# A fused two-block transformer kernel: order of the sparse attention's units, its softmax and two modulation sums beside the output projection

## The chip, the cores and the metric

The kernel runs on one core of one Trainium2 chip. The metric is device time in microseconds (us) of the whole program. A core has a tensor engine (PE, with its weight loads shown as PEld), a vector engine (DVE), a scalar engine (ACT), GpSimd (POOL, hardly used here) and a queue that issues loads (SP). Each engine runs its own list of instructions in order; they meet at semaphores.

## What is computed

Two transformer blocks over 256 tokens of width 1024, all in fp32. Only the first block's mixer matters here:

```python
mod = silu(c) @ ada_w + ada_b
sh1, sc1, g1, sh2, sc2, g2 = split(mod, 6)
h = rmsnorm(x, norm_mix_w) * (1 + sc1) + sh1
proj = h @ w_in                       # hq hf hi hg | sq sk sv iq ik iw | cu
o_a = hgrn2_mixer(...)                # recurrence, 512 wide
o_b = dsa_mixer(...)                  # top-64 keys per query, 4 heads of 64: 256 wide
o_c = conv_module(cu, ...)            # GLU, 31-tap causal conv, LayerNorm, swish: 256 wide
x = x + g1 * (concat([o_a, o_b, o_c]) @ w_out)
h = rmsnorm(x, norm_mlp_w) * (1 + sc2) + sh2
x = x + g2 * (square(relu(h @ mlp_w1)) @ mlp_w2)
```

In `dsa_mixer` a mask (`sel_bias`) with the 64 selected keys of each query is added to the scaled logits, and a softmax over the keys follows. The gate `g2` is needed only when the MLP's output is added.

## The kernel before

**Products.** A matrix product in fp32 is made from three products of rounded halves (`product3`, lines 582, 587 and 588): high by high, high by low, low by high. A weight tile of 128 x 2048 words arrives in one of five `raw` buffers. ACT rounds it into `w_hi` (line 1122, three buffers, called through `ahead`), and DVE makes `w_lo` as the difference (line 1514, called through `lo_ahead`). PE's `tile` waits for `weights_split`. `ahead(name, by)` makes the tiles up to `by` behind `name`. The activations are split in the same way by `split_input` (lines 1531 and 1532), and `split_mixed(j)` does it for quarter j of the concatenated mixer output `mixT`: quarters 0 and 1 are the recurrence, 2 is the sparse attention, 3 is the convolution.

**PSUM.** Eight banks. `PLAN` lists every result in the order in which PE makes it, and gives it a bank. PE's `begin(key)` waits until the former content of that bank has been read. `psum_full` counts results in the order of the plan. In the part with the convolution the banks go round; `wo` (the output projection) then holds banks 0 to 3, and the attention's results use banks 4 to 7.

**Modulation.** `modulation(u)` multiplies the silu of c with two `ada` tiles on PE (line 674) into a bank; `mod_copy(u)` on ACT copies it out; `modulation_sum(u)` adds the four partial rows up on PE (line 685 for u = 10, 11); `modulation_row(u)` on DVE adds the bias (line 1625). u = 10 and 11 are the two halves of g2. The queue SP loads the next weight tile into a `raw` buffer once its former tile was used: `wo0.1`, `wo1.0`, `wo1.1` and `m1_0.0` take the buffers of `ada20` to `ada23`, which modulations 10 and 11 read.

**The stretch in question**, at about 218 to 305 us:

- PE: convolution half 0 (line 857), modulations 10 and 11, convolution half 1, its mean (865), transposes of the recurrence (871), its variance `cvar` (877), the two modulation sums (685), then the attention beside the projection, `row_half("wo", 2, None)`, the transposes of the MLP's input (657) and the MLP's `m1` tiles.
- The attention has four units i: units 0 and 1 are query block 0 (128 keys), units 2 and 3 query block 1 (256 keys), each with two heads. L is the logits (782), T the transposes of the probabilities (764), O their product with the values (771). "rows j half" are 12 products of the projection with quarter j; quarters run in the order 0, 1, 3, 2, since quarter 2 needs all four O. PE's order before: L0, L1, rows 0 and 1 (48 products), L2, T0, L3, T1, O0, T2, O1, T3, O2, rows 3 first half, O3, rows 3 second half, rows 2.
- DVE: for each unit the mask is added (1588), the maximum taken (1592), and the reciprocal of the sum (1596); O is copied to `mixT` (1631). Around them: the convolution's mean (1832) and square (1835), `cvar` plus epsilon (1843), the splits of quarters 0 and 1, its LayerNorm (1851 to 1856), `modulation_row` 10 and 11 (1625), its product with the sigmoid (1863), the split of quarter 3 in step 1 of the softmax.
- ACT: the taps of the convolution (1193), the copies of the convolution's halves (1286, 1292), the exponentials (1147), the division by the sum (1157), the copy of T (1170).

After quarter 2 DVE splits two weight tiles and adds the projection to x (`gated_residual`, lines 1871 and 1875); the norm and the MLP follow.

Of the kernel before, what the change touches and what calls it, by code (L numbers as in the profile page):

```python
# [24 lines left out]
ALU = mybir.AluOpType  # L25
ACT = mybir.ActivationFunctionType
AX = mybir.AxisListType

P = 128
# [110 lines left out]


ROW_STAGES = {"wo": (0, 1, 3, 2), "o0": (2, 3, 0, 1), "o1": (0, 1, 2, 3)}
DSA_ROWS = [(1, 0, 0), (1, 0, 1), (1, 1, 0), (1, 1, 1), (5, 3, 0), (6, 3, 1)]
MLA_ROWS = [(2, 2, 0), (3, 2, 1), (4, 3, 0), (6, 3, 1), (8, 0, 0), (9, 0, 1)]
FOX_ROWS = [(9, 0, 0), (10, 0, 1), (12, 1, 0), (13, 1, 1), (16, 2, 0), (17, 2, 1)]

# [40 lines left out]
def psum_plan():  # L187
# [38 lines left out]
    for s in range(9):  # L226
# [6 lines left out]
        if 2 <= s <= 7:  # L233
            one(("mod", s + 2), PART_BANKS)
    plan.extend([("sc", t, j) for t in range(TT) for j in range(4)])
    plan.extend([("hgo", 0), ("hgo", 1)])
    plan.extend([("conv", 0), ("mod", 10), ("mod", 11), ("conv", 1), ("cmean",), ("hgt", 0), ("hgt", 1), ("cvar",),
                 ("ms", 10), ("ms", 11)])
    within(range(BANKS))

    def beside_rows(stage, order):
# [4 lines left out]
            plan.append((stage, t, n))  # L246
            banks_of.append(ROW_BANKS[i])

    beside_rows("wo", unit_order("dsa", 4, DSA_ROWS))
    transposes("mlp")  # L250
    for i in range(8):
        gemm(f"m1_{i}")
# [53 lines left out]
def bank(*key):  # L306
    return PLAN_BANKS[USE[key]]
# [7 lines left out]
def build(nc, x_in, wstream, pcol_in, prow_in, const_in, p_in, out):  # L315
    ctx = ExitStack()
    with ctx:
# [236 lines left out]
        def _(pe):  # L554
# [295 lines left out]
            for c in range(2):  # L850
                if c:
                    modulation(10)
                    modulation(11)
                pe.wait_ge(taps_made, c + 1)
                b = begin("conv", c)
                for j in range(31):
                    last = mm(b[:, 0:T], tap_matrix(c, j), hpad[:, c * 286 + j:c * 286 + j + T],
                              start=j == 0, stop=j == 30)
                last.then_inc(psum_full, 1)
# [7 lines left out]
            for t in range(TT):  # L867
                pe.wait_ge(o_normed, t + 1)
                b = begin("hgt", t)
                for h in range(4):  # L870
                    last = nc.tensor.transpose(b[:, h * P:(h + 1) * P],
                                               q_hg[:, t * 512 + h * P:t * 512 + (h + 1) * P], ident)
                last.then_inc(psum_full, 1)
            pe.wait_ge(conv_sq_ready, 1)
            b = begin("cvar")
            for c in range(2):
                last = mm(b[:, 0:T], avg[:, :], conv[:, c * T:(c + 1) * T], start=c == 0, stop=c == 1)
            last.then_inc(psum_full, 1)
            modulation_sum(10)
            modulation_sum(11)  # L880
            in_sbuf("sqk", 0)
            in_sbuf("sqk", 1)
            in_sbuf("sv")
            attention("dsa", 4, two_in_rows(sqT, skT),
                      lambda h, m: sv[:, m * T + h * 64:m * T + (h + 1) * 64], probs_ready, 0,
                      unit_order("dsa", 4, DSA_ROWS), "wo")
            row_half("wo", 2, None)

            to_feature_form("mlp", 2)
            for i in range(8):  # L890
# [173 lines left out]
        def _(act):  # L1064
# [22 lines left out]
            def warm_root(n):  # L1087
                A(table_use[:, n:n + 1], ones[:, 0:1], ACT.Sqrt)
# [36 lines left out]
            def bank_of(name, *key):  # L1125
# [8 lines left out]
                    ahead(name)  # L1134
                return wait_full(*key)

            def softmax(name, heads, base, beside=None):

                us = units(heads)
                for i in range(len(us) + 2):  # L1140
                    if i < len(us):
                        K = (us[i][2] + 1) * P
                        act.wait_ge(logits_ready, base + i + 1)
                        m = 2 * (i % 4)
                        for hh in range(2):
                            L = unit_logits[i % 4][:, hh * K:(hh + 1) * K]
                            last = A(L, L, ACT.Exp, bias=negmax[:, m + hh:m + hh + 1],  # L1147
                                     accum_out=rowsum[:, m + hh:m + hh + 1])
                        last.then_inc(exp_done, 1)
                    if 0 <= i - 1 < len(us):  # L1150

                        K = (us[i - 1][2] + 1) * P
                        m = 2 * ((i - 1) % 4)
                        act.wait_ge(rinv_ready, base + i)
                        for hh in range(2):
                            L = unit_logits[(i - 1) % 4][:, hh * K:(hh + 1) * K]
                            last = A(L, L, ACT.Copy, scale=rinv[:, m + hh:m + hh + 1])
                        last.then_inc(probs_ready, 1)
                    if i >= 2:
                        transposed(name, us, i - 2)  # L1160
                    if beside:
                        beside(i)
# [123 lines left out]
            done(A(conv[:, 0:T], b[:, 0:T], ACT.Identity, bias=col("cv_b", 0)), "conv", 0)  # L1286
            ahead("hi.1", 1)
            mod_copy(10)
            mod_copy(11)
            ahead("hi.1", 2)  # L1290
            b = wait_full("conv", 1)
            done(A(conv[:, T:2 * T], b[:, 0:T], ACT.Identity, bias=col("cv_b", 1)), "conv", 1)
            warm_root(15)
            act.wait_ge(bank_read[bank("cvar")], read("cvar"))
            A(hpad[:, 0:T], hpad[:, 0:T], ACT.Sqrt).then_inc(root_ready, 1)
            act.wait_ge(conv_scaled, 1)
            for c in range(2):
                last = A(conv_d[:, c * T:(c + 1) * T], conv[:, c * T:(c + 1) * T], ACT.Sigmoid)
            last.then_inc(conv_sig_done, 1)
            row_tile_at = {1: "wo0.0", 4: "wo0.1"}  # L1300
            softmax("dsa", 4, 0, lambda i: ahead(row_tile_at[i]) if i in row_tile_at else None)

            def residual_squares(first):
                for i in range(4):
# [182 lines left out]
        def _(dve):  # L1487
# [68 lines left out]
            def rms_norm(n, pieces=1):  # L1556
# [9 lines left out]
                        .then_inc(xn_ready, 1)  # L1566
                own(xn_ready, TT)

            def softmax(name, heads, base, bias, scale, c0, beside, tiles):
                us = units(heads)  # L1570
                n = len(us)
                for i in range(n + 3):
                    if name == "fox" and 1 <= i <= 6:
                        lo_ahead(f"{FOX_UPPER[i - 1][0]}.{FOX_UPPER[i - 1][1]}")
                    if i < n:
                        g, par, t = us[i]
                        K = (t + 1) * P
                        m = 2 * (i % 4)
                        b = wait_full(name, "L", i)
                        L = unit_logits[i % 4][:, 0:2 * K].rearrange("p (h k) -> p h k", h=2)  # L1580
                        if name == "fox":
                            for hh in range(2):
                                h = 4 * g + par + 2 * hh
                                last = V.scalar_tensor_tensor(out=L[:, hh, :], in0=b[:, hh * K:(hh + 1) * K],
                                                              scalar=dtok[:, t * 16 + h:t * 16 + h + 1],
                                                              in1=bias(t), op0=ALU.add, op1=ALU.add)
                        else:
                            last = V.scalar_tensor_tensor(
                                out=L, in0=b[:, 0:2 * K].rearrange("p (h k) -> p h k", h=2), scalar=scale,
                                in1=bias(t).unsqueeze(1).to_broadcast([P, 2, K]), op0=ALU.mult, op1=ALU.add)  # L1590
                        done(last, name, "L", i)
                        V.tensor_reduce(negmax[:, m:m + 2], L, AX.X, ALU.max, negate=True).then_inc(logits_ready, 1)  # L1592
                    if 0 <= i - 1 < n:
                        m = 2 * ((i - 1) % 4)
                        dve.wait_ge(exp_done, base_exp[0] + i)
                        V.reciprocal(rinv[:, m:m + 2], rowsum[:, m:m + 2]).then_inc(rinv_ready, 1)
                    for j, outputs in beside.get(i, ()):

                        for u in range(outputs):
                            wait_done(name, "O", u)  # L1600
                        split_mixed(j)
                    if i in tiles:
                        lo_ahead(tiles[i], 0)
                    if 0 <= i - 3 < n:
                        unit_output(name, us, i - 3, c0)
                for i in range(n):
                    wait_done(name, "O", i)
                base_exp[0] += n
# [245 lines left out]
            for c in range(2):  # L1854
# [2 lines left out]
                                       ALU.mult, ALU.add)  # L1857
            last.then_inc(conv_scaled, 1)
            own(conv_scaled)
            modulation_row(10, gate_rows[10])  # L1860
            modulation_row(11, gate_rows[11])
            dve.wait_ge(conv_sig_done, 1)
            V.tensor_tensor(mixT[:, 6:8, :], c2(conv), c2(conv_d), ALU.mult).then_inc(conv_out_ready, 1)
            own(conv_out_ready)
            softmax("dsa", 4, 0, lambda t: sel_bias[t][:, 0:(t + 1) * P], 0.125, 4, {1: [(3, 0)]},
                    {3: "wo1.0"})

            def gated_residual(stage, gate_row, tmp):
                for i, (t, n) in enumerate([(t, n) for t in range(TT) for n in range(2)]):
# [15 lines left out]
            for n in range(16):  # L1885
                key = (f"m1_{n // 2}", n % 2)
                lo_ahead(f"m1_{n // 2}.{n % 2}")
                wait_done(*key)
                v = product[n % 2]
                hs = slice(2 * n * T, (2 * n + 2) * T)  # L1890
                link(V.tensor_tensor(v, act_out[n % 2], act_out[n % 2], ALU.mult))
                link(V.tensor_copy(hid_hi[:, hs], v))
                V.tensor_tensor(hid_lo[:, hs], v, hid_hi[:, hs].bitcast(F32), ALU.subtract).then_inc(hid_split, 1)
                own(hid_split)
# [376 lines left out]
```

## Time and profile before

| | us |
|---|---|
| median of 3 runs | 1299.59 (1299.54 to 1299.69) |
| the profiled execution's own time | 1301.13 |
| its span in the trace | 1299.3 |
| mean granted PE clock in it | 0.934 of full |

All rows below are of the one profiled execution. A granted clock of 1.00 is 2.4 GHz and 0.50 is 1.2 GHz. A row of a timeline has the start, the duration and, in brackets, how long the engine was idle before it and what ended that.

### The profile page before, as it was taken

Reading aid. Unit: us, or ns where it says so; the run is one execution under the profiler, and the core shown is the slowest. Engines: PE = TensorE matmul, PEld = TensorE weight load, DVE = VectorE, ACT = ScalarE, POOL = GpSimd, SP = SyncE. Lnnn points to the kernel's source line nnn. Section 1 sums busy time; section 2 is a strip of 40 time slices with the busy share of each in tenths; the row PEclk is TensorE's granted clock in tenths of the full one; section 3 lists DMA queues with packets and bytes.
Section 4 is the critical chain, followed back from the end, with each engine's and each line's share of the span. In section 5 each row is a group of like instructions: output and inputs, shape, how many; then the busy total and the mean of one; then the engine's idle time right before and its main releaser. Section 6 shows DMA issues by size and latency. Waiting matters only on the chain.

```text
span 1299.3 us, 18592 instructions
## 1 busy us (share of the span) xinstructions
PE 1163.6 (90%) x7908; PEld 1045.8 (80%) x7908; DVE 754.8 (58%) x932; ACT 546.4 (42%) x755; POOL 0.2 (0%) x4
## 2 busy tenths in 40 slices
PE   4879989779999989947879999987999979999997
PEld 2879778559998879946679998886987659999887
DVE  2565556756775455366575665486344457566557
ACT  4562227244443334384543333344444444333333
POOL 0000000000000000000000000000000000000000
PEclk7788999888999998978999999998998979999999
DMA  9522764123555535410235555535431115455551
GB/s 387 229 83 98 287 229 177 61 90 132 193 180 185 193 128 215 150 66 33 98 118 176 194 176 184 193 130 211 147 114 68 63 67 183 175 193 177 192 182 34
DMA packets 33698, 200.95 MB, mean 155 GB/s; under 512 B 3152, under 2 KB 4688, under 8 KB 11984
## 3 DMA queue, kind: packets, MB, share of 16 engines
q1 hardware_dynamic: 32048, 190.30, 40.3%
q10 hardware_dynamic: 1568, 9.46, 1.9%
q8 instruction: 63, 1.03, 0.3%
q14 instruction: 19, 0.16, 0.0%
HBM read 198.70 MB, written 1.05 MB: 154 GB/s over the span
## 4 chain that ended last, share of the span: by engine, by line
PE 71%; DVE 16%; ACT 6%; DMA 4%; issue 2%; ACTq 0%; SPq 0%; DVEq 0%
PE bank L582 21%; PE bank L587 20%; PE bank L588 20%; DMA raw<-wstream 4%; DVE w_lo L1514 4%; PE bank L771 2%; DVE hT_lo L1532 2%; ACT w_hi L1122 1%; PE bank L1030 1%; DVE hT_hi L1531 1%; PE bank L764 1%; PE bank L1029 1%; PE bank L657 1%; PE bank L706 1%; PE bank L674 1%
## 5 line engine op out<-in xcount | busy, mean ns | idle before, releaser
L1514 DVE TENSOR_TENSOR w_lo<-raw,w_hi 128x2048 fp32r<-128x2048 f32 (+1 forms) x159 | 358.2, 2257 | 191.6 <-ACT w_hi L1122 184.5
L1122 ACT ACTIVATE w_hi<-raw 128x2048 fp32r<-128x2048 f32 (+1 forms) x159 | 299.4, 1885 | 280.0 <-PE bank L582 237.7
L582 PE MATMUL bank<-hT_hi,w_hi 128*128 128x256 f32 (+1 forms) x1360 | 392.5, 289 | 20.0 <-DVE w_lo L1514 11.0
L587 PE MATMUL bank<-hT_lo,w_hi 128*128 128x256 f32 (+1 forms) x1360 | 390.0, 287 | 0.0
L588 PE MATMUL bank<-hT_hi,w_lo 128*128 128x256 f32 (+1 forms) x1360 | 389.5, 286 | 0.0
L582 PEld LDWEIGHTS bank<-hT_hi,w_hi 128*128 128x128 f32 (+1 forms) x1360 | 264.9, 195 | 24.5 <-DVE w_lo L1514 12.5
L587 PEld LDWEIGHTS bank<-hT_lo,w_hi 128*128 128x128 f32 (+1 forms) x1360 | 265.1, 195 | 0.1
L588 PEld LDWEIGHTS bank<-hT_hi,w_lo 128*128 128x128 f32 (+1 forms) x1360 | 264.8, 195 | 0.2
L582 PE MATMUL bank<-w_hi,hT_hi 128*128 128x256 f32 (+3 forms) x448 | 148.3, 331 | 32.0 <-DVE w_lo L1514 12.1
L587 PE MATMUL bank<-w_lo,hT_hi 128*128 128x256 f32 (+3 forms) x448 | 144.3, 322 | 0.0
L588 PE MATMUL bank<-w_hi,hT_lo 128*128 128x256 f32 (+3 forms) x448 | 143.7, 321 | 0.0
L582 PEld LDWEIGHTS bank<-w_hi,hT_hi 128*128 128x128 f32 x448 | 92.6, 207 | 42.7 <-issue 18.6
L582 PE MATMUL bank<-w_hi,hid_hi 128*128 128x512 f32 x304 | 118.3, 389 | 0.0
L587 PE MATMUL bank<-w_lo,hid_hi 128*128 128x512 f32 x304 | 118.3, 389 | 0.0
L588 PE MATMUL bank<-w_hi,hid_lo 128*128 128x512 f32 x304 | 118.3, 389 | 0.0
L588 PEld LDWEIGHTS bank<-w_hi,hT_lo 128*128 128x128 f32 x448 | 92.2, 206 | 5.0
L587 PEld LDWEIGHTS bank<-w_lo,hT_hi 128*128 128x128 f32 x448 | 92.7, 207 | 4.2
L587 PEld LDWEIGHTS bank<-w_lo,hid_hi 128*128 128x128 f32 x304 | 57.1, 188 | 11.8
L582 PEld LDWEIGHTS bank<-w_hi,hid_hi 128*128 128x128 f32 x304 | 57.1, 188 | 11.8
L588 PEld LDWEIGHTS bank<-w_hi,hid_lo 128*128 128x128 f32 x304 | 57.1, 188 | 11.8
L1147 ACT ACTIVATE arena<-arena,tiny 128x128 f32<-128x128 f32 (+1 forms) x56 | 25.0, 447 | 72.0 <-DVE tiny L1592 71.9
L1465 ACT ACTIVATE arena<-bank 128x512 f32<-128x512 f32 x22 | 13.1, 597 | 78.0 <-PE bank L588 78.0
(264 smaller groups left out, 1099.4 us busy)
## 6 DMA issues: line engine op xcount, KB each, us to landing
raw<-wstream SPq DMA_DIRECT2D x179, 1024.0 KB, 4.8
arena<-prow ACTq DMA_DIRECT2D x2, 2560.0 KB, 10.4
x_res<-x ACTq DMA_DIRECT2D x1, 1024.0 KB, 14.5
rows<-prow ACTq DMA_DIRECT2D x2, 512.0 KB, 24.0
out<-x_res SPq DMA_DIRECT2D x4, 256.0 KB, 2.1
const_sb<-const ACTq DMA_DIRECT2D x1, 872.0 KB, 18.6
raw<-wstream SPq DMA_DIRECT2D x1, 768.0 KB, 4.1
raw<-wstream SPq DMA_DIRECT2D x1, 544.0 KB, 3.8
```

The costliest lines, as they stand in the source:

```text
L582: ins = mm(o, a[0], b[0], start=start, stop=False)
L587: mm(o, a[0], b[1], start=False, stop=False)
L588: return mm(o, a[1], b[0], start=False, stop=stop)
L657: last = nc.tensor.transpose(banks[j][:, c * T + t * P:c * T + (t + 1) * P], (x if stage == "ple" else xn)[:, t, (2 * j + c) * P:(2 * j + ...
L674: last = mm(b[32 * g:32 * g + 32, j * T:(j + 1) * T], csil[:, k:k + 1].to_broadcast([P, 32]), w[:, k, :], start=half == 0, stop=half == 1)
L706: last = mm(b[:, i * P:(i + 1) * P], lhsT, rhs, start=True, stop=True)
L771: last = mm(b[par * 64:par * 64 + 64, hh * P:(hh + 1) * P], values(4 * g + par + 2 * hh, m), pT_[:, (hh * nb + m) * P:(hh * nb + m + 1) * ...
L1122: A(w_hi[n % HI][:, 0:m], raw[:, slot % RAW, 0:m], ACT.Copy).then_inc(weights_rounded, 1)
L1147: last = A(L, L, ACT.Exp, bias=negmax[:, m + hh:m + hh + 1], accum_out=rowsum[:, m + hh:m + hh + 1])
L1465: A(act_out[i % 2], b[:, :], ACT.Sigmoid).then_inc(silu_sig_done, 1)
L1514: V.tensor_tensor(w_lo[slot][:, 0:m], raw[:, slot, 0:m], w_hi[n % HI][:, 0:m].bitcast(F32), ALU.subtract).then_inc(weights_split, 1)
L1532: V.tensor_tensor(hT_lo[:, s], src, hT_hi[:, s].bitcast(F32), ALU.subtract).then_inc(input_split, 1)
```

## The change

1. PE makes all four units' logits first, then 48 row products, then T0 and T1, rows 3 first half, O0 and O1, T2 and T3, rows 3 second half, O2 and O3. `rows 2` follows as before.
2. ACT's and DVE's softmax of this attention is written out. DVE takes the maxima of units 0, 1, 2, then reciprocals 0 and 1, the convolution's last product, the split of quarter 3, the maximum of unit 3, the split of `wo1.0`, reciprocals 2 and 3, outputs 0 and 1, the split of `wo1.1`, outputs 2 and 3. ACT rounds `wo1.0` behind the exponentials of units 2 and 3, and `wo1.1` behind the copies of T0 and T1.
3. `modulation(11)` moves on PE from ahead of convolution half 1 to behind the transposes of the recurrence, ahead of `cvar`; `mod_copy(11)` moves behind the copy of convolution half 1.
4. The sums of modulations 10 and 11 move on PE behind `rows 2`, and their two rows on DVE into the MLP's first step, behind the split of `m1_0.1`.

```diff
+DSA_ORDER = [("dsa", "L", 0), ("dsa", "L", 1), ("dsa", "L", 2), ("dsa", "L", 3),
+             ("rows", 0, 0), ("rows", 0, 1), ("rows", 1, 0), ("rows", 1, 1),
+             ("dsa", "T", 0), ("dsa", "T", 1), ("rows", 3, 0), ("dsa", "O", 0), ("dsa", "O", 1),
+             ("dsa", "T", 2), ("dsa", "T", 3), ("rows", 3, 1), ("dsa", "O", 2), ("dsa", "O", 3)]
-    plan.extend([("conv", 0), ("mod", 10), ("mod", 11), ("conv", 1), ("cmean",), ("hgt", 0), ("hgt", 1), ("cvar",),
-                 ("ms", 10), ("ms", 11)])
+    plan.extend([("conv", 0), ("mod", 10), ("conv", 1), ("cmean",), ("hgt", 0), ("hgt", 1), ("mod", 11), ("cvar",)])
-    beside_rows("wo", unit_order("dsa", 4, DSA_ROWS))
+    beside_rows("wo", DSA_ORDER)
+    plan.extend([("ms", 10), ("ms", 11)])
# PE
                     modulation(10)
-                    modulation(11)
...
+            modulation(11)
             pe.wait_ge(conv_sq_ready, 1)
...
-            modulation_sum(10)
-            modulation_sum(11)
...
             row_half("wo", 2, None)
+            modulation_sum(10)
+            modulation_sum(11)
# ACT
             mod_copy(10)
-            mod_copy(11)
             ahead("hi.1", 2)
             b = wait_full("conv", 1)
...
             warm_root(15)
+            mod_copy(11)
...
-            row_tile_at = {1: "wo0.0", 4: "wo0.1"}
-            softmax("dsa", 4, 0, lambda i: ahead(row_tile_at[i]) if i in row_tile_at else None)
+            us = units(4)
+            unit_exp(us, 0, 0)
+            unit_exp(us, 1, 0)
+            unit_normalise(us, 0, 0)
+            unit_normalise(us, 1, 0)
+            unit_exp(us, 2, 0)
+            unit_exp(us, 3, 0)
+            ahead("wo0.0", 2)
+            unit_normalise(us, 2, 0)
+            unit_normalise(us, 3, 0)
+            transposed("dsa", us, 0)
+            transposed("dsa", us, 1)
+            ahead("wo0.1", 2)
+            transposed("dsa", us, 2)
+            transposed("dsa", us, 3)
# DVE
-            modulation_row(10, gate_rows[10])
-            modulation_row(11, gate_rows[11])
+            us = units(4)
+            selected = lambda t: sel_bias[t][:, 0:(t + 1) * P]
+            unit_max("dsa", us, 0, selected, 0.125)
+            unit_max("dsa", us, 1, selected, 0.125)
+            unit_max("dsa", us, 2, selected, 0.125)
+            unit_rinv(0)
+            unit_rinv(1)
             dve.wait_ge(conv_sig_done, 1)
             V.tensor_tensor(mixT[:, 6:8, :], c2(conv), c2(conv_d), ALU.mult).then_inc(conv_out_ready, 1)
             own(conv_out_ready)
-            softmax("dsa", 4, 0, lambda t: sel_bias[t][:, 0:(t + 1) * P], 0.125, 4, {1: [(3, 0)]},
-                    {3: "wo1.0"})
+            split_mixed(3)
+            unit_max("dsa", us, 3, selected, 0.125)
+            lo_ahead("wo1.0", 0)
+            unit_rinv(2)
+            unit_rinv(3)
+            unit_output("dsa", us, 0, 4)
+            unit_output("dsa", us, 1, 4)
+            lo_ahead("wo1.1", 0)
+            unit_output("dsa", us, 2, 4)
+            unit_output("dsa", us, 3, 4)
...
                 lo_ahead(f"m1_{n // 2}.{n % 2}")
+                if n == 0:
+                    modulation_row(10, gate_rows[10])
+                    modulation_row(11, gate_rows[11])
```

`unit_exp`, `unit_normalise`, `unit_max` and `unit_rinv` hold the bodies of the former loops, unchanged; the other attentions still call `softmax`, which now calls these.

## Rows read from the trace of the kernel before

**Rows 1.** The page: the span, PE's clock in 40 slices, the shares of the chain that ended last

```profile
span 1299.3 us, 18592 instructions
...
PEclk7788999888999998978999999998998979999999
...
PE 71%; DVE 16%; ACT 6%; DMA 4%; issue 2%; ACTq 0%; SPq 0%; DVEq 0%
```

**Rows 2.** Timeline of PE, 218 to 250 us

```profile
218.24 3.66 PE L674 MATMUL bank<-raw,tiny 128*32 128x256 f32 x64
222.39 13.65 PE L857 MATMUL bank<-arena 128*128 128x256 f32 x62 [0.49 <-ACT arena L1193]
236.65 1.10 PE L865 MATMUL bank<-arena,avg 128*128 128x256 f32 x4 [0.61 <-issue]
...
239.93 1.13 PE L877 MATMUL bank<-arena,avg 128*128 128x256 f32 x4 [1.30 <-DVE arena L1835]
240.90 1.88 PE L685 MATMUL bank<-arena 128*128 128x512 f32 x4
242.71 0.72 PE L782 MATMUL bank<-arena 64*128 64x128 f32 x8
249.25 0.76 PE L582 MATMUL bank<-w_hi,hT_hi 128*128 128x512 f32 x1 [5.82 <-DVE arena L1625]
```

**Rows 3.** Timeline of ACT, 247 to 255 us

```profile
247.48 0.72 ACT L1298 ACTIVATE arena<-arena 128x256 f32<-128x256 f32 x2 [3.94 <-DVE arena L1856]
248.22 1.28 ACT L1147 ACT_TABLE_LOAD   x1
...
252.72 1.89 ACT L1122 ACTIVATE w_hi<-raw 128x2048 fp32r<-128x2048 f32 x1
```

**Rows 4.** Timeline of DVE, 238 to 265 us

```profile
238.40 0.68 DVE L1832 TENSOR_TENSOR arena<-arena,bank 128x512 f32<-128x512 f32 x1
...
241.36 0.42 DVE L1843 TENSOR_SCALAR arena<-bank 128x256 f32<-128x256 f32 x1
...
247.48 1.42 DVE L1625 TENSOR_TENSOR arena<-bank,arena 128x512 f32<-128x512 f32 x2
...
264.04 0.69 DVE L1588 SCALAR_TENSOR_TENSOR arena<-bank,arena 128x512 f32<-128x512 f32 x1 [11.35 <-PE bank L782]
```

**Rows 5.** The chain that ended last, 265 to 285 us: start, duration, what

```profile
265.49 1.09 ACT arena L1147 x4
...
272.53 1.90 PE bank L771 x8
...
277.63 1.03 PE bank L771 x8
...
280.44 4.49 DVE w_lo L1514 x2
```

**Rows 6.** Busy time by windows: length, PE, PEld, DVE, ACT, POOL, granted clock, DMA

```profile
249.20:254.40 5.20, 5.15 (x12) 4.11 (x13) 3.19 (x8) 4.13 (x12) 0.00 (x0) 0.50 0.00 0
254.40:262.50 8.10, 8.10 (x37) 6.59 (x36) 0.00 (x0) 0.21 (x1) 0.00 (x0) 1.00 0.38 131
...
903.25:906.40 3.15, 3.15 (x14) 3.15 (x15) 2.68 (x2) 1.91 (x1) 0.00 (x0) 0.50 0.43 143
```

**Rows 7.** Timeline of PE at five other waits

```profile
190.40 0.58 PE L582 MATMUL bank<-w_hi,hT_hi 128*128 128x256 f32 x1 [3.03 <-DVE w_lo L1514]
...
293.68 3.64 PE L657 MATMUL bank<-const_sb,xn 128*128 128x128 f32 x16 [5.14 <-DVE xn L1565]
...
552.88 0.47 PE L582 MATMUL bank<-w_hi,hT_hi 128*128 128x512 f32 x1 [2.65 <-DVE w_lo L1514]
...
903.25 0.58 PE L582 MATMUL bank<-hT_hi,w_hi 128*128 128x256 f32 x1 [2.31 <-DVE w_lo L1514]
...
1055.12 0.47 PE L582 MATMUL bank<-w_hi,hT_hi 128*128 128x512 f32 x1 [2.10 <-DVE hT_lo L1532]
```

**Rows 8.** Timeline of DVE in the first step of the MLP

```profile
306.82 0.69 DVE L1891 TENSOR_TENSOR arena<-arena 128x512 f32<-128x512 f32 x1 [2.57 <-ACT arena L1321]
```

More of the change, by code:

```diff
@@ L142 @@
 ROW_STAGES = {"wo": (0, 1, 3, 2), "o0": (2, 3, 0, 1), "o1": (0, 1, 2, 3)}
-DSA_ROWS = [(1, 0, 0), (1, 0, 1), (1, 1, 0), (1, 1, 1), (5, 3, 0), (6, 3, 1)]
+DSA_ORDER = [("dsa", "L", 0), ("dsa", "L", 1), ("dsa", "L", 2), ("dsa", "L", 3),
+             ("rows", 0, 0), ("rows", 0, 1), ("rows", 1, 0), ("rows", 1, 1),
+             ("dsa", "T", 0), ("dsa", "T", 1), ("rows", 3, 0), ("dsa", "O", 0), ("dsa", "O", 1),
+             ("dsa", "T", 2), ("dsa", "T", 3), ("rows", 3, 1), ("dsa", "O", 2), ("dsa", "O", 3)]
 MLA_ROWS = [(2, 2, 0), (3, 2, 1), (4, 3, 0), (6, 3, 1), (8, 0, 0), (9, 0, 1)]
@@ L885, in _ @@
                       lambda h, m: sv[:, m * T + h * 64:m * T + (h + 1) * 64], probs_ready, 0,
-                      unit_order("dsa", 4, DSA_ROWS), "wo")
+                      DSA_ORDER, "wo")
             row_half("wo", 2, None)
+            modulation_sum(10)
+            modulation_sum(11)
             to_feature_form("mlp", 2)
@@ L1135, in bank_of, with unit_exp, unit_normalise @@
                 return wait_full(*key)
+            def unit_exp(us, i, base):
+                K = (us[i][2] + 1) * P
+                act.wait_ge(logits_ready, base + i + 1)
+                m = 2 * (i % 4)
+                for hh in range(2):
+                    L = unit_logits[i % 4][:, hh * K:(hh + 1) * K]
+                    last = A(L, L, ACT.Exp, bias=negmax[:, m + hh:m + hh + 1],
+                             accum_out=rowsum[:, m + hh:m + hh + 1])
+                last.then_inc(exp_done, 1)
+            def unit_normalise(us, i, base):
+                K = (us[i][2] + 1) * P
+                m = 2 * (i % 4)
+                act.wait_ge(rinv_ready, base + i + 1)
+                for hh in range(2):
+                    L = unit_logits[i % 4][:, hh * K:(hh + 1) * K]
+                    last = A(L, L, ACT.Copy, scale=rinv[:, m + hh:m + hh + 1])
+                last.then_inc(probs_ready, 1)
             def softmax(name, heads, base, beside=None):
@@ L1141, in softmax @@
                     if i < len(us):
[L1142 to L1149, printed above, removed]
-                    if 0 <= i - 1 < len(us):
[L1152 to L1158, printed above, removed]
+                        unit_exp(us, i, base)
+                    if 0 <= i - 1 < len(us):
+                        unit_normalise(us, i - 1, base)
                     if i >= 2:
@@ L1567, in rms_norm, with unit_max, unit_rinv @@
                 own(xn_ready, TT)
+            def unit_max(name, us, i, bias, scale):
+                g, par, t = us[i]
+                K = (t + 1) * P
+                m = 2 * (i % 4)
+                b = wait_full(name, "L", i)
+                L = unit_logits[i % 4][:, 0:2 * K].rearrange("p (h k) -> p h k", h=2)
+                if name == "fox":
+                    for hh in range(2):
+                        h = 4 * g + par + 2 * hh
+                        last = V.scalar_tensor_tensor(out=L[:, hh, :], in0=b[:, hh * K:(hh + 1) * K],
+                                                      scalar=dtok[:, t * 16 + h:t * 16 + h + 1],
+                                                      in1=bias(t), op0=ALU.add, op1=ALU.add)
+                else:
+                    last = V.scalar_tensor_tensor(
+                        out=L, in0=b[:, 0:2 * K].rearrange("p (h k) -> p h k", h=2), scalar=scale,
+                        in1=bias(t).unsqueeze(1).to_broadcast([P, 2, K]), op0=ALU.mult, op1=ALU.add)
+                done(last, name, "L", i)
+                V.tensor_reduce(negmax[:, m:m + 2], L, AX.X, ALU.max, negate=True).then_inc(logits_ready, 1)
+            def unit_rinv(i):
+                m = 2 * (i % 4)
+                dve.wait_ge(exp_done, base_exp[0] + i + 1)
+                V.reciprocal(rinv[:, m:m + 2], rowsum[:, m:m + 2]).then_inc(rinv_ready, 1)
             def softmax(name, heads, base, bias, scale, c0, beside, tiles):
@@ L1575, in softmax @@
                     if i < n:
[L1576 to L1592, printed above, removed]
+                        unit_max(name, us, i, bias, scale)
                     if 0 <= i - 1 < n:
-                        m = 2 * ((i - 1) % 4)
-                        dve.wait_ge(exp_done, base_exp[0] + i)
-                        V.reciprocal(rinv[:, m:m + 2], rowsum[:, m:m + 2]).then_inc(rinv_ready, 1)
+                        unit_rinv(i - 1)
                     for j, outputs in beside.get(i, ()):
@@ L1864, in _ @@
             own(conv_out_ready)
-            softmax("dsa", 4, 0, lambda t: sel_bias[t][:, 0:(t + 1) * P], 0.125, 4, {1: [(3, 0)]},
-                    {3: "wo1.0"})
+            split_mixed(3)
[8 more added lines that the diff above has]
+            unit_output("dsa", us, 3, 4)
+            for i in range(4):
+                wait_done("dsa", "O", i)
+            base_exp[0] += 4
             def gated_residual(stage, gate_row, tmp):
```

## The prediction

> **What bounds the kernel now.** I read the page first: of the chain that ended last, 71% is PE [rows 1]. The kernel as a whole is bound by PE, so a change of order can only win where PE stands still or runs at half clock. The timeline of PE around the change shows both. After the first two units' logits (242.71 us) PE does nothing for 5.82 us, until DVE's line 1625 is over [rows 2]. Line 1625 is `modulation_row` 10 and 11, which reads the banks of the modulation sums; by the plan they are banks 2 and 3, which the projection takes. So the first product of the projection waits for a gate that nobody needs yet. The windows show what follows that idle time: the granted clock is 0.50 from 249.2 to 254.4, where 12 products take 5.2 us (0.43 each), and 1.00 behind it, where 36 take 8.1 us (0.225 each) [rows 6]. The timeline of DVE then shows DVE idle for 11.35 us, waiting for the logits of unit 2, which PE makes behind 48 row products [rows 4]. The chain from there is a relay (maximum, exponential, division, transposes, O) with little beside it, partly at half clock: O2 takes 1.90 us where O3, the same work, later takes 1.03 [rows 5]. At its end DVE splits two weight tiles in a row (4.49 us) before it may add the projection to x, which begins when they end, at 284.96 (280.44 and 4.49 and an issue gap) [rows 5]. Behind that point the chain is the same in both kernels, so I take the start of this addition as the finish line.
>
> **The new order, up to the logits.** With modulation 11 moved, PE runs only modulation 10 between the convolution's halves: half of 3.66 us, from 218.24 to 220.07. Half 1 must wait for its taps, which ACT ends no earlier than before; half 1 starts at 222.39, released by them [rows 2]. PE's gap there grows from 0.49 us to 2.32. The gap itself costs nothing, since half 1 starts at the same time. The clock behind it may cost. In this trace an idle time of 2.31 us was followed by 3.15 us at clock 0.50, and one of 2.65 us by no fall (the first product behind it took 0.47 us, where that behind 5.82 us took 0.76) [rows 2, 6, 7]. I take the fall, of the length seen at 903.25: half of about 3.4 us, 1.7 us lost; bounds are 0 and, for a low stretch twice as long, 3.4. Half 1 then ends 1.7 us later. DVE takes its mean at 238.40, 0.65 us after PE had made it (236.65 and 1.10), so 0.65 us of it is covered for DVE [rows 2, 4]. But `cvar` now stands behind modulation 11 (1.83 us) on PE, and PE is late by the whole 1.7 us. Without the loss: transposes end at about 238.7, modulation 11 at 240.5, `cvar` at 241.65, and DVE reads it at 241.7 instead of 241.36, 0.35 us later [rows 2, 4]. With it, 2.05 us later. ACT's wait for modulation 11 stands ahead of its wait for `cvar`, so it holds nothing up. Reciprocal and LayerNorm behind it are unchanged: from 241.36 to their end took 6.12 us (line 1625 starts at 247.48) [rows 4]; now they end at 249.5.
>
> A rule of the Trainium skill speaks to this gap. The page "TensorE: Matmul & The Clock Gate", Part 1, says that the clock goes to its lower level after an idle window. Taken by its words a gap with work on both sides, as this one, would cost nothing, and the sum would be 1.7 us lower; the idle time of 2.65 us agrees with it and that of 2.31 us does not. The trace decides by a small majority: of seven idle times of PE between 1.9 and 3.1 us behind its first 120 us, from 190.40 to 1055.12, six had a low clock next to them, all but that at 552.88 [rows 7].
>
> **The loads.** SP is in order. The load of `wo1.1` waits for the first half of modulation 11 and that of `m1_0.0` for the second: they move back by some 19 us, as modulation 11 does (220.1 to 238.7). ACT rounds these two tiles only at about 264 and later, which leaves 23 us behind the end of modulation 11. I take nothing; if that room were gone, all later loads would queue behind it.
>
> **Rows 0 and 1.** Logits of units 2 and 3 follow 0 and 1 at once, about 0.7 and 2.3 us, into banks 6 and 7, which DVE has read by then. The projection's banks are now held by modulation 11, `cvar`, convolution half 0 and modulation 10, all read by 244. So rows start at 244.9, or 246.6 with the loss, at full clock, since PE is no longer idle: 48 x 0.227 = 10.9 us, and T0 and T1 take 0.8. PE is free at 258.3. This removes the 5.82 us wait and 12 x 0.2 = 2.4 us of half clock [rows 2, 6].
>
> **The softmax on DVE and ACT** is the new path. From 249.5: maxima 0 and 1 take 1.6 us (units of 128 keys), maximum 2 takes 1.4 (two instructions of 0.69 [rows 4]). ACT has its sigmoid (0.72), the load of the table (1.28) and two exponential pairs of 0.8 to do, 3.6 us [rows 3], so reciprocal 1 falls at 249.5 + 3.95. Then the product with the sigmoid 0.7, the split of quarter 3 1.15, maximum 3 1.4: 7.2 us, at 256.7. Exponential 3 takes ACT 1.0 (1.09 for four records [rows 5]) and the rounding of `wo1.0` 1.9 [rows 3]; DVE's split of it takes 2.3 (half of 4.49 [rows 5]). `wo1.0` is split at 249.5 + 12.45 = 262.0. Before, ACT rounded that tile at 252.72, 22 us before PE took it (272.53 and 1.90) [rows 3, 5]. So a new wait appears: PE stands still from 258.3 to 262.0, 3.7 us. I expect the clock to be low behind it as it was behind 5.82, 5.14 and 2.31 us [rows 2, 7]. The loss lies between 0 and 3.4 us (the low stretch between none and twice the one at 903.25); I take that of 249.2 to 254.4, 2.4 us.
>
> **From there to the finish line.** Rows 3 first half 12 x 0.43 = 5.1 us; O0 and O1 1.1; T2 and T3 1.1 (four records each where O2 and O3 have eight); rows 3 second half 2.75; O2 and O3 2.1 (1.03 each [rows 5]). ACT's divisions and copies and its rounding of `wo1.1`, and DVE's split of it, lie beside these. That gives 274.2. The last output copy 0.45 and the split of quarter 2 1.15: 275.8. PE starts rows 2, and DVE has only `m1_0.0` left to split, 2.3 us instead of 4.49: the addition starts at 278.1. Rows 2 deliver their first block 1.5 us after their start, so they are ahead of it. 284.96 - 278.1 = 6.85 us gained.
>
> **The moved sums.** On PE the two sums are 1.88 us [rows 2]. They stand behind rows 2 (over at 281.4) and wait for banks 0 and 1, which DVE reads by 280.4. The norm gives PE work at 286.7; before, PE was idle for 5.14 us there [rows 7]. Cost nothing; 1.9 us if that cover were gone. The clock fell there before and the remaining 3.4 us should let it fall again; if not, the transposes and the first MLP products at half clock are spared, up to 3 us. On DVE the two rows are 1.42 us, in a step where DVE was idle for 2.57 us [rows 4, 8]: nothing. Later PSUM banks move on by two, all round the same eight: nothing.
>
> **Sum.** 6.8 us. The profiled execution took 1301.13 us with a span of 1299.3, so it would take 1294.3. The three runs have a median of 1299.59, 1.5 below it; the same gain gives 1292.8.
>
> **Rivals.**
> - *The clock holds in the gap before convolution half 1.* For it: the 2.65 us case, and the skill's rule above. Against: 2.31 us at 903.25 [rows 7]. 1.7 us better, 1291.1. If it holds behind the new wait too, 2.4 more: 1288.7. Chances 0.22 and 0.06.
> - *Low clocks last longer, or the shift of everything behind moves other waits into them.* Behind 300 us many slices of the page have a clock below 9 tenths [rows 1]; the shift may move such a stretch onto dense products. At 1.7 us for a stretch, two of them are 3.4: 1296.2. Chance 0.16.
> - *The relay of the softmax eats the gain.* The path now runs through one chain over DVE and ACT before `wo1.0` is split. If each hand-over costs some 0.3 us more than I count over its dozen steps, PE waits about 3.8 us longer and with other losses the time is 1298 to 1299.5, no change. Chance 0.07.
> - *Slower: the clock stays low through convolution half 1.* Its 13.65 us of products at full clock would take 27.3, 12 us more than I count: 1304.8. It decides from some 17 us of low clock in this stretch, 3.4 of which are in my sum (6.8 us of loss is 13.6 us of low clock). For it: nothing with dense work in this trace; the low stretch of 249.2 ended after 5.2 us of products [rows 6]. Chance 0.04.
> - The forecast itself has 0.45.
>
> **Numbers.** The range from 1288.5 to 1297.5 leaves out the slower case, most of the eaten gain and the tail of the case with both clocks held. 0.2% is 2.6 us, about what a measurement of this kernel can tell from no change. Faster than 1297.0: forecast, both clock cases and most of the third, 0.88. Within 0.2%: 0.08. Slower: 0.04.
>
> **What the changed profile would show.** The first row product at 245 to 247 with no idle time of several us before it; clock 1.00 under the first 48; no 11 us idle in DVE; a PE wait of 3 to 4 us for DVE line 1514 behind T1, with 0.50 behind it; the addition to x at 277 to 279; the sums inside PE's wait for the norm; 0.50 for some 3.4 us in convolution half 1. The prediction is wrong if `wo1.0` is split well after 263, if the low stretches have other lengths, or if the MLP's first steps wait for a load.

## The result and the profile after

The changed kernel takes 1290.10 us (median of 5 runs, 1286.00 to 1292.86), against 1299.54 for the kernel before in the same comparison: a ratio of 0.9929, with a 95% interval of 0.9908 to 0.9951. It is 9.4 us faster by the medians; the prediction said 6.8 and 1292.8. The profiled execution took 1290.97 us, with a span of 1289.2.

The page of the changed kernel: the span, and PE's clock in 40 slices, which answer to [rows 1].

```profile
span 1289.2 us, 18591 instructions
...
PEclk8788999989999998969989999998998989999999
```

The timeline of PE in the changed kernel (start, duration, and in brackets the idle time ahead and what ended it); its lines answer to [rows 2]. Line numbers have moved: 859 is the convolution, 677 a modulation, 880 `cvar`, 785 the logits, 767 the transposes T, 774 the outputs O, 585 the first of three products, 688 the sums, 660 the transposes of the MLP's input. In the kernels of the experiments they differ by a few lines again.

```profile
217.28 1.93 PE L677 MATMUL bank<-raw,tiny 128*32 128x256 f32 x32
221.42 15.34 PE L859 MATMUL bank<-arena 128*128 128x256 f32 x62 [2.21 <-ACT arena L1203]
237.37 1.10 PE L867 MATMUL bank<-arena,avg 128*128 128x256 f32 x4 [0.61 <-issue]
...
239.28 1.93 PE L677 MATMUL bank<-raw,tiny 128*32 128x256 f32 x32
241.14 1.13 PE L880 MATMUL bank<-arena,avg 128*128 128x256 f32 x4
242.20 1.68 PE L785 MATMUL bank<-arena 64*128 64x128 f32 x16
244.14 0.47 PE L585 MATMUL bank<-w_hi,hT_hi 128*128 128x512 f32 x1 [0.26 <-DVE hT_lo L1555]
...
255.11 0.60 PE L767 MATMUL bank<-const_sb,arena 128*128 128x128 f32 x4
260.92 0.80 PE L585 MATMUL bank<-w_hi,hT_hi 128*128 128x512 f32 x1 [5.21 <-DVE w_lo L1537]
...
270.73 1.58 PE L774 MATMUL bank<-arena 128*64 128x128 f32 x16
...
279.73 1.88 PE L688 MATMUL bank<-arena 128*128 128x512 f32 x4
285.13 1.94 PE L660 MATMUL bank<-const_sb,xn 128*128 128x128 f32 x16 [3.52 <-DVE xn L1588]
288.87 0.36 PE L585 MATMUL bank<-hT_hi,w_hi 128*128 128x256 f32 x1 [1.81 <-DVE hT_lo L1555]
```

Read from the top: the gap ahead of convolution half 1 has grown to 2.21 us, and half 1 takes 15.34 us where it took 13.65. The idle time of 5.82 us ahead of the first row product has shrunk to 0.26. A new one of 5.21 us stands behind T1; it ends when DVE has split `wo1.0`. The sums lie behind the rows, and PE is idle behind them all the same until the norm gives it work.

The windows of the changed kernel, with the columns of [rows 6]: convolution half 1 at its start, the new wait, and what follows it.

```profile
222.00:225.40 3.40, 3.40 (x10) 2.68 (x9) 3.16 (x11) 3.40 (x3) 0.00 (x0) 0.50 1.04 394
256.00:260.50 4.50, 0.00 (x0) 0.00 (x0) 1.93 (x1) 2.54 (x5) 0.00 (x0) 0.90 0.00 0
260.50:265.50 5.00, 4.58 (x11) 3.62 (x12) 0.50 (x3) 4.04 (x7) 0.00 (x0) 0.50 0.50 180
```

The clock is 0.50 behind both gaps; behind the first it falls only some 0.6 us after half 1 has begun. The new wait brings back low-clock products of the same kind as the old one had.

The timeline of DVE in the changed kernel, answering to [rows 4] and, by its last line, to [rows 8].

```profile
242.38 0.42 DVE L1874 TENSOR_SCALAR arena<-bank 128x256 f32<-128x256 f32 x1 [0.94 <-PE bank L880]
...
247.73 0.74 DVE L1887 TENSOR_SCALAR arena<-arena,pcol_sb 128x256 f32<-128x256 f32 x2
...
254.93 0.69 DVE L1610 TENSOR_REDUCE tiny<-arena 128x2 f32<-128x512 f32 x1
258.57 2.29 DVE L1537 TENSOR_TENSOR w_lo<-raw,w_hi 128x2048 fp32r<-128x2048 f32 x1 [2.96 <-ACT w_hi L1125]
...
276.42 0.69 DVE L1918 TENSOR_TENSOR arena<-bank,rows 128x512 f32<-128x512 f32 x1
...
297.10 0.69 DVE L1941 TENSOR_TENSOR arena<-arena 128x512 f32<-128x512 f32 x1 [1.16 <-ACT arena L1344]
```

`cvar` is now waited for (0.94 us). Behind the maximum of unit 3 DVE waits 2.96 us for ACT's rounding of `wo1.0`, splits it, and so releases PE. The two rows of the gate cost nothing in the MLP's first step: DVE is still idle for 1.16 us there, of the former 2.57.

**Where the time went.** Convolution half 1 starts at another moment in every profile (217.0 to 222.4 us) although nothing ahead of it was changed, so I measure from that start, H. The addition to x starts at 276.42 in the changed kernel. In the kernel before the addition to x starts at 284.96, and the first product of the MLP is this line of PE's timeline.

```profile
298.50 0.55 PE L582 MATMUL bank<-hT_hi,w_hi 128*128 128x256 f32 x1 [1.18 <-DVE hT_lo L1532]
```

| | before | after | gained |
|---|---|---|---|
| start to H | 222.39 | 221.42 | 0.97 |
| H to the addition | 62.57 | 55.00 | 7.57 |
| the addition to the MLP's first product | 13.54 | 12.45 | 1.09 |
| from there to the end of the span | 1000.80 | 1000.33 | 0.47 |
| span | 1299.3 | 1289.2 | 10.1 |

### The profile page after: what moved, and what is told of

The parts are those of the page before. It is cut to its first block, busy times and chain, and to the rows that moved or that the text cites. A ratio compares the mean times of both kernels' runs of the same rounds, so it can differ in the third digit from the quotient of the medians.

```text
span 1289.2 us, 18591 instructions
## 1 busy us (share of the span) xinstructions
PE 1154.4 (90%) x7908; PEld 1040.3 (81%) x7908; DVE 754.9 (59%) x932; ACT 546.4 (42%) x755; POOL 0.2 (0%) x4
## 4 chain that ended last, share of the span: by engine, by line
PE 72%; DVE 14%; ACT 6%; DMA 4%; issue 2%; ACTq 0%; SPq 0%; DVEq 0%
PE bank L585 21%; PE bank L591 21%; PE bank L590 21%; DMA raw<-wstream 4%; DVE w_lo L1537 4%; PE bank L774 2%; DVE hT_lo L1555 2%; ACT w_hi L1125 2%; PE bank L1033 1%; PE bank L859 1%; PE bank L1032 1%; DVE hT_hi L1554 1%; PE bank L660 1%; PE bank L767 1%; PE bank L677 1%
```

## The experiments

Eight kernels, in two groups of four; each group shares its runs of the kernel before. Times are medians. Ratios are to the kernel before of the group (1297.49 us in the first group, 1296.57 in the second), with their 95% intervals; they are worked out apart from the medians and are not exactly the quotients of the medians. The edits are shown in part: the entries of `PLAN`, and with modulation 11 its `mod_copy`, move with the lines shown.

**1. The sums alone.** The kernel before with this edit only:

```diff
-            modulation_sum(10)
-            modulation_sum(11)
             in_sbuf("sqk", 0)
...
             row_half("wo", 2, None)
+            modulation_sum(10)
+            modulation_sum(11)
...
-            modulation_row(10, gate_rows[10])
-            modulation_row(11, gate_rows[11])
...
                 lo_ahead(f"m1_{n // 2}.{n % 2}")
+                if n == 0:
+                    modulation_row(10, gate_rows[10])
+                    modulation_row(11, gate_rows[11])
```

> The kernel before with one part of the change: the sums of modulations 10 and 11 behind the projection on PE and their rows in the MLP's first step on DVE. Modulation 11, the order of the attention and its softmax as before. Theory 1 (each part alone removes one of two things that lie one behind the other, so either is worth nearly the whole): the rows start at about 243.5 us instead of 249.25, at full clock, so unit 2's logits come 8 us earlier and all behind them: about 8 us faster, 1291. Rival (the order is what gains): the relay of units 2 and 3 still stands behind the 48 row products with PE idle in it; the sums give back only the half clock, 2.4 us: 1297.

Measured 1286.49 us, ratio 0.9921 (0.9902 to 0.9941). PE's timeline, and then DVE's:

```profile
219.97 13.65 PE L857 MATMUL bank<-arena 128*128 128x256 f32 x62 [0.49 <-ACT arena L1193]
...
240.70 0.47 PE L582 MATMUL bank<-w_hi,hT_hi 128*128 128x512 f32 x1 [1.40 <-DVE hT_lo L1532]
251.79 1.13 PE L782 MATMUL bank<-arena 64*128 64x256 f32 x4
```

```profile
253.03 0.69 DVE L1588 SCALAR_TENSOR_TENSOR arena<-bank,arena 128x512 f32<-128x512 f32 x1 [3.37 <-PE bank L782]
...
268.56 4.49 DVE L1514 TENSOR_TENSOR w_lo<-raw,w_hi 128x2048 fp32r<-128x2048 f32 x2
273.08 0.69 DVE L1869 TENSOR_TENSOR arena<-bank,rows 128x512 f32<-128x512 f32 x1
```

The rows wait only for their input's split now, and the logits of unit 2 come 31.8 us behind H instead of 40.4. Of these 8.6 us, 6.1 are the earlier start of the rows (20.7 us behind H instead of 26.9) and 2.5 the half clock that is gone, as theory 1 has it, and all behind them moves too. DVE still has the relay and the pair of splits (4.49 us). H to the addition is 53.1 us and H to the MLP 66.1; both are less than in the changed kernel (55.0 and 67.5). The rival falls.

**2. The order alone.** The changed kernel with the sums and rows in their old places and modulation 11 ahead of half 1:

```diff
+            modulation_sum(10)
+            modulation_sum(11)
             in_sbuf("sqk", 0)
...
             row_half("wo", 2, None)
-            modulation_sum(10)
-            modulation_sum(11)
...
+            modulation_row(10, gate_rows[10])
+            modulation_row(11, gate_rows[11])
             us = units(4)
```

> The changed order and the written-out softmax alone: the two sums stay on PE ahead of the attention, the two rows on DVE ahead of its maxima, modulation 11 ahead of convolution half 1. Theory 1: the rows still start at 249.3 us behind an idle time of some 5 us and at clock 0.50, but the whole softmax runs beside them; wo1.0 is split at about 261.3, before PE is done with 48 products and T1 (263.4), so the new wait of 5.2 us is gone: the addition to x starts at about 277 instead of 285, 8 us faster, 1291.7. Rival (the hand-over of the banks is what gains): the wait for the sums stays, so the time is within 2 us of before.

Measured 1291.84 us, ratio 0.9954 (0.9936 to 0.9972). PE's timeline:

```profile
247.33 0.76 PE L585 MATMUL bank<-w_hi,hT_hi 128*128 128x512 f32 x1 [4.87 <-DVE arena L1656]
...
260.67 0.60 PE L767 MATMUL bank<-const_sb,arena 128*128 128x128 f32 x4
261.02 0.48 PE L585 MATMUL bank<-w_hi,hT_hi 128*128 128x512 f32 x1
```

The wait for DVE's line 1656 (`modulation_row`) and the low clock behind it are there as before, and rows 3 follow T1 with no wait at all, since the tile was split long before. H to the addition is 53.6 us, 9.0 less than before, and H to the MLP 68.1, which is 8.05 less. The 1 us between the two is lost behind the addition's start: PE makes rows 2 partly at low clock (mean 0.65 from 271.8 to 275.0), and DVE's timeline has a wait for them.

```profile
276.49 0.69 DVE L1920 TENSOR_TENSOR arena<-bank,rows 128x512 f32<-128x512 f32 x1 [0.98 <-PE bank L591]
```

In the whole runs the gain is 5.7 us by the medians, somewhat less than the 8 expected. The rival, a time within 2 us of before, falls.

**3. All but modulation 11.**

```diff
                     modulation(10)
+                    modulation(11)
...
-            modulation(11)
             pe.wait_ge(conv_sq_ready, 1)
```

> The whole change but for modulation 11, which stays ahead of convolution half 1 (with its copy). Theory 1: no gap of 2.2 us before half 1, its products take 13.65 us and not 15.34, and cvar follows the transposes at once: everything behind is 2 us earlier than in the changed kernel, 1288. Rival: the 2 us are covered, or given back by clocks further on: 1290, as the changed kernel.

Measured 1286.63 us, ratio 0.9914 (0.9897 to 0.9930). PE's timeline:

```profile
218.97 13.66 PE L860 MATMUL bank<-arena 128*128 128x256 f32 x62 [0.49 <-ACT arena L1203]
...
239.70 0.47 PE L585 MATMUL bank<-w_hi,hT_hi 128*128 128x512 f32 x1 [0.44 <-DVE hT_lo L1555]
...
256.48 0.79 PE L585 MATMUL bank<-w_hi,hT_hi 128*128 128x512 f32 x1 [5.18 <-DVE w_lo L1537]
```

The first row product stands 20.73 us behind H, against 22.72 in the changed kernel: the 2 us that were expected. H to the addition is 52.4 us against 55.0. So the move of modulation 11 gives time away. The intervals of the whole-run ratios (0.9908 to 0.9951 for the changed kernel) overlap; the trace tells the two apart, the runs alone don't quite.

**4. Modulation 11 alone**, in the kernel before:

```diff
                     modulation(10)
-                    modulation(11)
...
+            modulation(11)
             pe.wait_ge(conv_sq_ready, 1)
```

> The kernel before with modulation 11 alone moved behind the transposes of the recurrence, ahead of cvar. Theory 1: it costs 0.35 us by its place and 1.7 by the clock in convolution half 1, so 2 us slower than before, 1301.6, with half 1 at 15.3 us and clock 0.50 for about 3.4 us in it. Rival: the clock's fall is a matter of the moment and is absent in the profile; 0.35 us slower, 1300.0.

Measured 1301.30 us, ratio 1.0022 (1.0008 to 1.0035): a little slower. PE's timeline:

```profile
220.28 15.34 PE L856 MATMUL bank<-arena 128*128 128x256 f32 x62 [2.21 <-ACT arena L1193]
```

The window of 220.9 to 224.3 us has a granted clock of 0.51. H to DVE's reading of `cvar` is 20.97 us against 18.97 before, 2.0 us more, and H to the MLP 2.5 us more. Theory 1 holds, in size too by the trace; the medians of the whole runs stand 3.8 us apart.

**5. The changed kernel again**, for the second group.

> The changed kernel once more, on the chip of this group: what stands against the other three. Both theories: 0.7% below before, with a PE wait of 5.2 us for the split of wo1.0 and clock 0.50 behind it.

Measured 1290.33 us, ratio 0.9945 (0.9925 to 0.9964). The interval overlaps that of the first comparison; by the medians the gain is 6.2 us here and was 9.4 there. The wait for `wo1.0` is 5.18 us, and H to the addition 54.95.

**6. The tile earlier.**

```diff
# ACT
             A(hpad[:, 0:T], hpad[:, 0:T], ACT.Sqrt).then_inc(root_ready, 1)
+            ahead("wo0.0", 2)
             act.wait_ge(conv_scaled, 1)
...
             unit_exp(us, 3, 0)
-            ahead("wo0.0", 2)
# DVE
             split_mixed(3)
+            lo_ahead("wo1.0", 0)
             unit_max("dsa", us, 3, selected, 0.125)
-            lo_ahead("wo1.0", 0)
```

> The changed kernel, but wo1.0 is rounded by ACT in its idle time ahead of the convolution's sigmoid, and split by DVE behind quarter 3, ahead of the maximum of unit 3. Theory 1 (the tile is what PE waits for behind T1): rows 3 start 4 us earlier (some 1 us of wait instead of 5.2) and at full clock; then O0 waits about 1.5 us for ACT, which copies T0 only behind the divisions of units 2 and 3; the addition to x starts some 4 to 5 us earlier: 0.35% below the changed kernel. Rival (the softmax itself is the chain, the tile was merely its last link): the wait moves to O0 and T3 in full, and the gain is under 2 us.

Measured 1283.10 us, ratio 0.9894 (0.9868 to 0.9920). PE's timeline:

```profile
217.03 13.66 PE L859 MATMUL bank<-arena 128*128 128x256 f32 x62 [2.22 <-ACT arena L1203]
...
250.48 0.50 PE L585 MATMUL bank<-w_hi,hT_hi 128*128 128x512 f32 x1 [0.81 <-DVE w_lo L1537]
...
254.88 0.89 PE L774 MATMUL bank<-arena 128*64 128x128 f32 x8 [1.39 <-ACT arena L1180]
```

The wait of 5.2 us is down to 0.81, the clock stays at 1.00 behind it (windows 250.4 to 254.0 and 254.8 to 261.0), and O0 waits 1.39 us for ACT's copy of T0, as expected. The rival falls: the tile was the wait, not the softmax. The first line holds something that I had not asked for: the same gap of 2.2 us ahead of half 1, and half 1 takes 13.66 us. Here the clock did not fall. H to the addition is 48.2 us; 1.7 us of what it has over the changed kernel's 55.0 come from this (DVE reads `cvar` 19.28 us behind H instead of 20.96), the rest, 5.2, from the edit. The profiled execution is one of the fastest of this kernel's six (1278.76 us; they range from 1278.63 to 1289.34), so its clocks are not typical ones.

**7. And T0 and T1 copied earlier.**

```diff
             unit_exp(us, 2, 0)
+            transposed("dsa", us, 0)
+            transposed("dsa", us, 1)
             unit_exp(us, 3, 0)
             unit_normalise(us, 2, 0)
             unit_normalise(us, 3, 0)
-            transposed("dsa", us, 0)
-            transposed("dsa", us, 1)
```

> As tile_early, and ACT copies T0 and T1 ahead of the exponential of unit 3. Theory 1: O0 and O1 follow rows 3 first half at once; no wait over 1.5 us from the first row product to the end of O3, clock 1.00 throughout; the addition starts some 7 us earlier than in the changed kernel: 0.5% below it. Rival: exponential 3 comes too late behind the copies, T3 waits, and it is no better than tile_early.

Measured 1285.42 us, ratio 0.9912 (0.9895 to 0.9930). PE's timeline:

```profile
218.47 15.34 PE L859 MATMUL bank<-arena 128*128 128x256 f32 x62 [2.21 <-ACT arena L1203]
...
253.60 0.50 PE L585 MATMUL bank<-w_hi,hT_hi 128*128 128x512 f32 x1 [0.81 <-DVE w_lo L1537]
...
256.54 0.66 PE L774 MATMUL bank<-arena 128*64 128x128 f32 x8
...
275.47 3.65 PE L660 MATMUL bank<-const_sb,xn 128*128 128x128 f32 x16 [3.52 <-DVE xn L1588]
```

The wait of O0 is gone. (The last line is the transposes of the MLP's input, told of at the end.) With half 1 slow again, H to the addition is 48.3 us, 6.7 less than in the changed kernel (7 expected). Whether this beats experiment 6 the whole runs can't tell: their intervals overlap and the medians stand the other way. From the first row product to the addition the trace has 25.56 us here and 27.11 in experiment 6, 1.55 us less; against the whole H to the addition this is hidden by the slow half 1.

**8. And modulation 11 back** (the edit of 3 on top of 7).

> As tile_copies, with modulation 11 ahead of convolution half 1 as in the kernel before. Theory 1: 2 us more, as from the changed kernel to the one with modulation 11 put back: 9 us below the changed kernel, 0.7%; 1.4% below before. Rival: with no other waits left PE's order is the bound and the 2 us are not seen.

Measured 1280.48 us, ratio 0.9873 (0.9854 to 0.9892), the lowest median of all, though its interval overlaps that of experiment 6. PE's timeline:

```profile
218.45 13.66 PE L860 MATMUL bank<-arena 128*128 128x256 f32 x62 [0.49 <-ACT arena L1203]
...
251.59 0.50 PE L585 MATMUL bank<-w_hi,hT_hi 128*128 128x512 f32 x1 [0.81 <-DVE w_lo L1537]
```

H to the addition is 46.3 us, 2.0 less than in 7, and theory 1 holds. This kernel beats the changed one by 9.85 us in the medians of one group, in which the changed one beats the one before by 6.2.

All stretches side by side, in us, from the profiles:

| kernel | H | H to first row product | H to addition | H to MLP |
|---|---|---|---|---|
| before | 222.39 | 26.86 | 62.57 | 76.11 |
| 4, modulation 11 alone | 220.28 | 28.86 | 65.05 | 78.59 |
| 2, order alone | 220.46 | 26.87 | 53.57 | 68.06 |
| 1, sums alone | 219.97 | 20.73 | 53.11 | 66.06 |
| changed | 221.42 | 22.72 | 55.00 | 67.45 |
| 5, changed, again | 221.39 | 22.72 | 54.95 | 67.41 |
| 3, changed, modulation 11 back | 218.97 | 20.73 | 52.44 | 65.10 |
| 6, tile earlier | 217.03 | 21.04 | 48.15 | 62.50 |
| 7, tile and copies earlier | 218.47 | 22.72 | 48.28 | 61.82 |
| 8, and modulation 11 back | 218.45 | 20.73 | 46.31 | 58.95 |

The last column holds clocks that no edit aimed at. In experiments 2 and 6 rows 2 fell to the low clock and the addition waited for PE by 0.98 and 0.87 us in all; in the five other profiles with the new order this did not happen. The transposes of the MLP's input took from 1.94 to 3.65 us. So a difference of 1 to 2 us that shows in this column alone is no sign of an edit.

## Why the prediction was right, and where its sizes were off

**The gap ahead of half 1.** Right in mechanism and size: 2.21 us of gap (2.32 said), 15.34 us for half 1 (1.7 more, as said, though the stretch at 903.25 that the prediction put at about 3.4 us has 3.15 us of products in its row [rows 6]), `cvar` read 20.96 us behind H where it was 18.97: 1.99 later (2.05 said). Experiments 3 and 4 show from both sides that it is the move of modulation 11 that costs this. It was a gamble all the same, since the clock held in one of five profiles with this gap (experiment 6). The rival in which it holds is real; the forecast was the likelier case. The prediction's count of six low clocks in seven idle times hangs in part on its lower bound of 1.9 us: an idle time of 1.89 us, at 644.97 in the kernel before, had clock 1.00 behind it. The rule of the Trainium skill that the prediction quotes ("TensorE: Matmul & The Clock Gate", Part 1) agrees with that one profile and not with the four others.

**The first rows.** The wait of 5.82 us and the low clock behind it are gone, as said. They start 22.72 us behind H, where I had 24.2: the logits of all four units took 1.68 us of PE by the record, not 3.0. This gained nothing, since the path lay in the softmax.

**The softmax as the path.** LayerNorm's end to the split of `wo1.0` took 12.4 us (248.47 to 260.86) where the sum had 12.45. The new wait is 5.21 us and not 3.7, since PE was ready earlier; its end came 39.4 us behind H, and 39.6 was said. The low clock behind it was there. Experiment 6 shows that this tile was the wait: split some 4 us earlier (33.4 us behind H, or 35.1 with the slow half 1 of experiment 7, where it was 39.4), 4.4 us of wait and the low clock were gone.

**To the finish line.** 55.0 us behind H against 55.7. The term that was too large is O: the pairs took 0.6 and 1.53 us on the chain where I had 1.1 and 2.1. Three of the signs named fell just outside their ranges in the profile: the first row product at 244.14 (245 to 247 said), the wait of 5.21 us (3 to 4), and the addition at 276.42 (277 to 279), of which 0.97 us is the earlier H.

**What the sum left out.** It ended at the addition and took the rest as equal. Of the 10.1 us between the spans 0.97 lie ahead of H, where nothing was changed, so that is luck; then there are 1.09 between the addition and the MLP, and 0.47 behind. The 1.09 is the bound that the prediction named and did not take: the transposes of the MLP's input ran at full clock (1.94 us where they took 3.64 [rows 7]) after an idle time of 3.52 us instead of 5.14. That stands for about 1.7 us of PE's time, of which a part is given back, since the MLP's first product then waited 1.81 us for a split, not 1.18. The edit does not make it certain: with the same idle time within 0.02 us the transposes took 1.94 us in experiment 5, 2.76 in 3, 2.74 in 8 and 3.65 in 7. In whole runs the forecast of 6.8 us stands between the two measured gains, 9.4 and 6.2 us.

**What I had not seen: the parts are not a sum.** The prediction credited the missing 5.82 us to the sums and the shorter end to the order. Experiments 1 and 2 show that each of them alone brings nearly all (10.05 and 8.05 us from H to the MLP), and both together 11.0 (experiment 3). The whole change, with modulation 11 moved, has 8.7, less than the sums alone; H to the addition says the same (7.6 against 9.5). In the new order PE waits either for the banks or for a tile at the end of the softmax. With the sums in their old place the banks come late, and the softmax and the tile are done meanwhile (experiment 2: no wait behind T1); with the banks early, PE gets to the tile before the softmax does (experiment 3: 5.18 us). Set side by side, experiments 1 and 3 have 1286.49 and 1286.63 us: once the sums are moved, the new order shows no gain in whole runs, until the tile is split earlier (experiments 6 to 8).

**The loads.** Moving the loads of `wo1.1` and `m1_0.0` back by 19 us cost nothing that is seen: no wait of PE or ACT in the stretch of the changed kernel is for a DMA.

**What stays open.** Why H differs by 5 us between profiles, and why the remainder behind the MLP's first product lies between 997.5 (experiment 6) and 1003.3 us (experiment 7) in code that is the same, was not tried. The low stretches fall at other places in each profile, which may be all of it. The runs of one kernel spread by 3 to 11 us (10.7 in experiment 6). Within every kernel's runs the slower ones have in the main the lower mean granted clock: in experiment 6 it is 0.948 at 1278.63 us and 0.941 at 1289.34, in the kernel before of the second group 0.942 at 1292.29 and 0.933 at 1300.24. So the clock goes with the spread; that it is all of the spread is not shown.

## What to carry to other kernels

When two edits each take a wait from the same stretch, the second may find its gain already spent: time each by itself before crediting it, and look for what is late next. A result that nobody needs soon should not hold banks that the next stage wants; its sum is best put where its engine waits anyway. And before a softmax is laid beside products, the weight tile that those products need must be made in the idle time of its engines and not behind the last exponential.

## What the runs showed of the hardware

An idle time of PE of 2.2 us, the same to 0.01 us in five profiles, was followed by a low clock in four of them and not in the fifth: half 1 took 15.34 us or 13.66. So what a gap of this length costs is not fixed by the code. The clock did not fall in the gap but with products already running: some 0.6 us into half 1 in the changed kernel and 1.4 us in experiment 7. An idle time of 1.90 us ahead of rows 2, the same in seven profiles, was followed by clock 1.00 in five, where the 24 products of rows 2 took 5.7 us, and by a low stretch in two, where they took 7.3 (experiments 2 and 6). An idle time of 3.52 us ahead of the MLP's transposes was followed by full clock in the changed kernel (16 transposes in 1.94 us), while in experiment 7 one of the same 3.52 us had them take 3.65.
